# The opening of a two-block transformer kernel: modulation rows moved on TensorE, the first projection chunk split by tokens

## Chip, cores and metric

The kernel runs on one core of a Trainium2 chip. The metric is the device time of one execution in microseconds (us); before the change it is 2401.89 us, the median of three runs (2400.64 to 2404.11). The core has five engines with queues of their own: TensorE (PE, with its weight loads listed apart as PEld), VectorE (DVE), ScalarE (ACT), GpSimd (POOL) and SyncE (SP), which here only issues DMAs. They meet through semaphores alone.

## The reference, cut to what matters

Two diffusion transformer blocks of two layers each run one behind the other on 512 latent tokens of width 1024; the first block also carries 256 context tokens. All is in float32. What the change touches is the beginning of the first block's first layer:

```python
def layer(x, cx, c_silu, cctx_silu, norm_w, ada_w, ada_b, w_in, ...):
    mod = c_silu @ ada_w + ada_b
    mod_c = cctx_silu @ ada_w + ada_b
    shift, scale, gate = jnp.split(mod, 3, axis=-1)
    hx = rmsnorm(x, norm_w) * (1 + scale[:, None, :]) + shift[:, None, :]
    hc = rmsnorm(cx, norm_w) * (1 + scale_c) + shift_c
    px = split_cols(hx @ w_in)
    pc = split_cols(hc @ w_in)
    ...
```

So before the first projection there must be a sum of squares over the 1024 features of each token, its root, and shift and scale, which are products of a vector of 1024 with a matrix of 1024 x 2048, once for the latent and once for the context condition.

## The kernel before

Features lie on the 128 partitions in eight chunks (c = 0 to 7), tokens along the free axis: 512 latent (`SEQ`) and 256 context tokens (`CTX`), 768 in all (`TOK`). Each product of float32 matrices is made of three matmuls of rounded parts: a weight panel is split into its rounded half (made by ACT, `round_panel1`) and the rest (made by DVE for the first two panels, L1958 to L1960, later by POOL); the modulated input h is split in the same way into `hs1[:, 0]` (rounded) and `hs1[:, 1]` (rest). The projection is made in blocks of 128 output features, and `block_chunk` (L2594) adds one chunk c to one block: for the parts (rounded, rounded), (rounded weight, rest of h), (rest of weight, rounded h) it makes one matmul of 512 columns and one of 256.

Every order is written out by hand, as one program per engine; a wait stops all that stands behind it on that engine.

**SP** issues the loads in a row: small vectors, matrices, x in four parts, modulation panels 0 and 1 of 1 MB (`stage_low`), the first two weight panels (`panels_first`, 0.5 MB each), modulation panels 2 to 7, and more.

**PE** begins at L2585 with 36 matmuls of an identity (`WARM_UP`; float32, so two records each), then sums the squares with one-column matmuls (`sum_squares`, L2439: the added squares of seven chunks first, then those of the last chunk), makes the first group of modulation rows (`mod_rows_of(0)`, L2413: two panels of 256 columns, 16 matmuls of 32 output rows each), spreads the roots over the partitions (`spread_roots`, L2563) and turns the rows into columns (`turn_mod(0)`, L2427). There are four such groups g of two panels; group g serves chunks 2g and 2g + 1. In the first block of the projection (L2660 to L2678) the groups 1 to 3 stand between the chunks: rows 1 ahead of chunk 0, turn 1 and rows 2 ahead of chunk 1, turn 2 ahead of chunk 2, rows 3 ahead of chunk 3, turn 3 ahead of chunk 4. Each chunk waits for the rest of h (`h_even` from DVE, `h_odd` from POOL) and then serves the blocks 0 and 1, six matmuls each.

**ACT** squares x, takes the root of the sums (L1555), then makes a small root (L1557), rounds panel 0, copies the rows out of PSUM (`take_rows(0)`, L1333), rounds panel 1, and takes the turned modulation (`take_mod`, L1324). In the loop over chunks (L1564) it adds the shift and rounds: for even chunks in one step per token range (L1584), for odd ones in two (L1575, L1581). Ahead of chunk 2 stand `take_rows(1)`, two `take_mod` and `take_rows(2)`, ahead of chunk 4 two `take_mod`, ahead of chunk 5 `take_rows(3)`; the last two `take_mod` stand within chunk 5.

**DVE** adds the squares (L1955), inverts the roots, makes the rests of panels 0 and 1 (L1960), and then per pair of chunks waits for `mod_taken` and makes shift and gain (`modulate`, L1962, with small additions at L1967). For each chunk it multiplies x by gain and root (L2035, 512 and 256 tokens; `hm_ready`), and after each odd chunk it makes the rest of the even chunk before it (L2041).

**POOL** makes the rest of h for the odd chunks (L1230).

## Time and profile before

| | us |
|---|---|
| median of three runs | 2401.89 |
| lowest and highest run | 2400.64, 2404.11 |
| the profiled execution's own time | 2404.52 |
| its span (first to last instruction) | 2402.4 |
| PE busy | 2345.2 |
| DVE, ACT, POOL busy | 1349.6, 1023.4, 470.7 |

All times below are in us from the start of the span. A timeline row gives start, duration, engine, line and operation, the tile written and the tiles read, the shape, the number of instructions merged into the row, and in brackets how long the engine sat idle before it and what released it. Float32 matmuls leave two records each, those on rounded parts one. Two instructions that follow one another on PE overlap by their tail, so a row of many is somewhat longer than the distance to the next row's start.

### The profile page before, as it was taken

The page shows a single profiled execution, that of the slowest core. Times are in us where ns is not written, and L with a number is a line of the kernel's source. Part 1 is how long each engine was busy: PE and PEld are TensorE (multiplying, and loading weights), DVE is VectorE, ACT ScalarE, POOL GpSimd, SP SyncE. Part 2 cuts the span into 40 slices and gives each one's busy share as a digit, 9 for nine tenths or more (in the row PEclk, how much of TensorE's full clock was granted, in tenths as well). Part 3 has the DMA queues.
Part 4 walks back from the last instruction along what each step waited for, and adds up shares of the span by engine and source line. Part 5 has one row for each costly group of instructions (what it writes and reads, how often), then busy time and mean ns, then how long its engine had stood idle before and what let it go on. Part 6 is the DMA issues. An engine that isn't in the chain of part 4 may idle for free.

```text
span 2402.4 us, 40532 instructions
## 1 busy us (share of the span) xinstructions
PE 2345.2 (98%) x16250; PEld 1943.8 (81%) x16250; DVE 1349.6 (56%) x2719; ACT 1023.4 (43%) x1808; POOL 470.7 (20%) x290
## 2 busy tenths in 40 slices
PE   8999999999999999999999999999999999999998
PEld 6888878788887888878787678888888768888887
DVE  5777675685238755767458644333337855433333
ACT  5673275632337625662454434222235544222222
POOL 2202212012342032203663320000014232000001
PEclk9999999999999999999999999999999999999999
DMA  7303413044133063407242122233232112323222
GB/s 299 141 2 132 167 53 142 2 159 150 60 125 141 2 225 105 150 2 276 90 142 71 62 79 85 83 105 105 81 107 89 62 55 69 108 80 119 96 76 74
DMA packets 64203, 250.55 MB, mean 104 GB/s; under 512 B 7408, under 2 KB 9968, under 8 KB 54544
## 3 DMA queue, kind: packets, MB, share of 16 engines
q1 hardware_dynamic: 61216, 236.10, 28.3%
q0 software_dynamic: 2592, 11.54, 1.5%
q8 instruction: 129, 2.11, 0.3%
q14 instruction: 58, 0.48, 0.1%
q10 hardware_dynamic: 208, 0.33, 0.0%
HBM read 243.67 MB, written 4.19 MB: 103 GB/s over the span
## 4 chain that ended last, share of the span: by engine, by line
PE 84%; ACT 5%; DVE 4%; issue 3%; POOL 2%; DVEq 1%; ACTq 0%; DMA 0%; SPq 0%; POOLq 0%
PE ps L2786 40%; PE ps L2601 21%; PE ps L2763 4%; PE ps L607 4%; PE ps L716 4%; ACT probs L922 3%; PE ps L657 3%; PE ps L701 1%; PE ps L2483 1%; PE ps L2580 1%; POOL split_panels_first L1191 1%; DVEq L805 1%; DVE ps L1944 1%; DVE ps L822 1%; PE ps L2528 1%
## 5 line engine op out<-in xcount | busy, mean ns | idle before, releaser
L2786 PE MATMUL ps<-h_split,split_panels 128*128 128x512 f32 x2928 | 686.1, 393 | 1.9 <-ACT projected L1693 0.8
L2786 PEld LDWEIGHTS ps<-h_split,split_panels 128*128 128x128 f32 x2928 | 545.4, 188 | 126.9 <-issue 14.1
L2601 PE MATMUL ps<-h_split_first,split_panels_first 128*128 128x512 f32 (+1 forms) x2772 | 535.7, 351 | 3.2 <-DVE h_split_first L2041 2.2
L2601 PEld LDWEIGHTS ps<-h_split_first,split_panels_first 128*128 128x128 f32 x2772 | 441.9, 189 | 72.4 <-issue 3.9
L2121 DVE TENSOR_TENSOR split_panels<-panels,split_panels 128x1024 fp32r<-128x1024 f32 (+2 forms) x171 | 191.6, 1121 | 297.3 <-ACT split_panels L1408 293.7
L1191 POOL TENSOR_TENSOR split_panels_first<-panels_first,split_panels_first 128x1024 fp32r<-128x1024 f32 (+2 forms) x102 | 225.2, 2208 | 676.7 <-ACT split_panels_first L1389 676.7
L1408 ACT ACTIVATE split_panels<-panels 128x1024 fp32r<-128x1024 f32 (+2 forms) x210 | 204.3, 974 | 343.0 <-PE ps L2786 341.4
L1944 DVE SCALAR_TENSOR_TENSOR ps<-modulation_panels,silu_c,ps 128x256 f32<-128x256 f32 x480 | 225.3, 488 | 30.0 <-issue 1.7
L2786 PE MATMUL ps<-ffn_hidden_split,split_panels 128*128 128x512 f32 x990 | 225.0, 389 | 0.0
L2786 PEld LDWEIGHTS ps<-ffn_hidden_split,split_panels 128*128 128x128 f32 x990 | 185.8, 188 | 38.6
L1209 POOL TENSOR_TENSOR probs_turned<-probs_turned,probs 128x512 f32<-128x512 f32 x30 | 42.4, 1412 | 760.1 <-ACT probs L1636 760.1
L607 PE MATMUL ps<-qkv 64*128 64x256 f32 (+1 forms) x1232 | 144.8, 362 | 4.5 <-ACT qkv L1470 2.7
L1389 ACT ACTIVATE split_panels_first<-panels_first 128x1024 fp32r<-128x1024 f32 (+2 forms) x104 | 102.9, 990 | 93.9 <-PE ps L2763 93.1
L922 ACT ACTIVATE probs<-ps,row_min 128x512 f32<-128x512 f32 (+6 forms) x192 | 122.1, 643 | 44.1 <-DVE row_min L822 34.0
L1221 POOL TENSOR_TENSOR split_panels<-panels,split_panels 128x1024 fp32r<-128x1024 f32 x39 | 94.3, 2419 | 170.0 <-ACT split_panels L1408 168.8
L2763 PE MATMUL ps<-gated_rounded,split_panels_first 128*128 128x512 f32 x504 | 123.7, 356 | 0.3 <-POOL split_panels_first L1191 0.3
L607 PEld LDWEIGHTS ps<-qkv 64*128 64x128 f32 x1232 | 99.6, 188 | 29.6 <-issue 22.7
L657 PEld LDWEIGHTS ps<-matrices,probs 64*128 64x128 f32 x2048 | 80.9, 139 | 47.3 <-ACT probs L922 42.2
L1468 ACT ACTIVATE qkv<-ps 128x512 f32<-128x512 f32 x38 | 36.3, 954 | 187.0 <-PE ps L2601 186.8
L657 PE MATMUL ps<-matrices,probs 64*128 64x64 f32 x2048 | 92.3, 227 | 19.3 <-ACT probs L922 17.4
L1820 ACT ACTIVATE probs<-ps 128x512 f32<-128x512 f32 x44 | 26.3, 598 | 181.4 <-PE ps L2786 181.3
L2375 DVE TENSOR_TENSOR probs<-probs,ps 128x512 f32<-128x512 f32 x44 | 30.3, 688 | 117.2 <-PE ps L2786 117.2
(313 smaller groups left out, 3071.2 us busy)
## 6 DMA issues: line engine op xcount, KB each, us to landing
modulation_panels<-in_ada SPq DMA_DIRECT2D x64, 1024.0 KB, 4.9
panels<-in_w SPq DMA_DIRECT2D x88, 512.0 KB, 3.2
panels_first<-in_in SPq DMA_DIRECT2D x72, 512.0 KB, 5.7
panels<-in_in SPq DMA_DIRECT2D x42, 512.0 KB, 3.2
panels_first<-in_out SPq DMA_DIRECT2D x32, 384.0 KB, 3.1
panels<-in_w SPq DMA_DIRECT2D x32, 384.0 KB, 3.1
panels<-in_w SPq DMA_DIRECT2D x32, 320.0 KB, 2.9
panels<-in_out SPq DMA_DIRECT2D x16, 512.0 KB, 3.2
```

What stands on the lines that cost most here:

```text
L607: last[e] = nc.tensor.matmul(scores_at(u, e, u["w"][e])[:, col:col + z - a], u["q"][e], u["k"][e][:, a:z], start=True, stop=True, skip_gro ...
L657: ins = [nc.tensor.transpose(to, src, ident[rows_of(half), HD * half:HD * half + HD]) for half, (to, src) in enumerate(two)]
L716: ins = nc.tensor.matmul(bank(b, 0, P)[rows_of(e)], v, turned_slot(ev, at0 + P)[:, at0:at0 + P], start=ev["first"] and j < 2, stop=ev["las ...
L922: nc.scalar.activation(probs[:, u["probs_at"], e, 0:w], scores_at(u, e, w), ACT.Exp, bias=row_min[:, s:s + 1], scale=scale, accum_out=row_ ...
L1191: nc.gpsimd.tensor_tensor(flat1(n, 1)[:, s], raw1[:, n % RAW1, s], flat1(n, 0)[:, s].bitcast(F32), ALU.subtract).then_inc(rest1_done, 1)
L1389: A_(flat1(n, 0)[:, s], raw1[:, n % RAW1, s], ACT.Copy).then_inc(rounded1, 1)
L1408: A_(flat(n, 0), raw[:, n % RAW, 0:panel_size(n)], ACT.Copy).then_inc(rounded, 1)
L1944: ins = V.scalar_tensor_tensor(out=adding if c < KC - 1 else products(k)[:, i, :], in0=w[:, c, :], scalar=v, in1=adding, op0=ALU.mult, op1 ...
L2121: V.tensor_tensor(flat(n, 1), raw[:, n % RAW, 0:panel_size(n)], flat(n, 0).bitcast(F32), ALU.subtract).then_inc(rest_done, 1)
L2601: ins = mm(at0, split1[:, s, w, c, :], hs1[:, h, c, lo:e], start=c == 0 and i == 0, stop=c == KC - 1 and i == 2)
L2763: ins = mm(bank(OUT_BANKS[j][o % 2], 0, e), split1[:, n % SPLIT1, w, c, :], u[:, uc, lo:lo + e], start=uc == 0 and i == 0, stop=uc == MIXC ...
L2786: ins = mm(out, split[:, n % SPLIT, a, c - base, :], moving(b, c), start=first and i == 0 and j == 0, stop=last and i == len(chunks) - 1 a ...
```

## The change

PE: 42 instead of 36 warm-up matmuls. The first group's rows are cut in two: panel 0 goes between the sums of the added squares and those of the last chunk, panel 1 behind them. Behind the first turn stand eight more matmuls of the identity (`SHORT_WAIT`). Block 0's chunks go through a new function, `first_chunk`, which waits only for the rounded h, makes the two parts that need the rounded h, waits for the rest and makes the third. Rows 1 move from ahead of chunk 0 to between its two blocks, rows 2 from ahead of chunk 1 to behind it, turn 2 to between the blocks of chunk 2; turn 1, rows 3 and turn 3 keep their places.

ACT: `take_rows(0)` moves ahead of the small root and the rounding of panel 0; `take_rows(2)` from ahead of chunk 2 to ahead of chunk 3. For chunk 0 the 512 latent tokens wait for a new semaphore, `scaled_first`, which DVE sets after its first product of chunk 0; the 256 context tokens wait for `hm_ready` as before.

```diff
-WARM_UP = 36
+WARM_UP = 42
+SHORT_WAIT = 8
...
                 if l == 0:
                     root(l, TOK // P)
+                    take_rows(0)
+                    round_panel1(0)
                     act.wait_ge(tiny_set, 1)
                     A_(weights_of_squares[:, :], weights_of_squares[:, :], ACT.Sqrt, bias=EPS)
-                    round_panel1(0)
-                    take_rows(0)
                     round_panel1(1)
...
-                    if c == 2:
+                    if c == 3:
                         take_rows(2)
+                    if c == 0:
+                        act.wait_ge(scaled_first, 1)
+                        A_(hs1[:, 0, c, 0:SEQ], hm1[:, c % 4, 0:SEQ], ACT.Identity, bias=mod1[:, l, c, 0:1])
                     act.wait_ge(hm_ready, KC * l + c + 1)
+                    if c == 0:
+                        A_(hs1[:, 0, c, SEQ:TOK], hm1[:, c % 4, SEQ:TOK], ACT.Identity, bias=mod1[:, l, c, 1:2]).then_inc(hh_ready, 1)
+                        continue
...
+                            if (c, j) == (0, 0):
+                                ins.then_inc(scaled_first, 1)
...
-            sum_squares(0, TOK // P)
             pe.wait_ge(silu_done, 3)
-            mod_rows_of(0)
+            sum_added_squares(0, TOK // P)
+            mod_rows_of(0, (0,))
+            sum_last_squares(0, TOK // P)
+            mod_rows_of(0, (1,))
             spread_roots(0, TOK // P)
             turn_mod(0)
+            for _ in range(SHORT_WAIT):
+                mm(bank(0, 0, P), ident, ident, start=True, stop=True)
...
+            def first_chunk(l, b, c):
+
+
+                k, s = NSEQ[l, b], main_no[IN1, l, b] % SPLIT1
+                pe.wait_ge(hh_ready, KC * l + c + 1)
+                for i, (w, h) in enumerate(((0, 0), (1, 0), (0, 1))):
+                    if i == 2:
+                        pe.wait_ge(h_odd if c % 2 else h_even, c // 2 + 1)
+                    for at0, lo, e in ((bank(k % 2), 0, SEQ), (bank(2 + k % 2, 0, CTX), SEQ, TOK)):
+                        ins = mm(at0, split1[:, s, w, c, :], hs1[:, h, c, lo:e], start=c == 0 and i == 0, stop=c == KC - 1 and i == 2)
...
                         pe.wait_ge(rest1_done, main_no[IN1, l, 1] + 1)
+                        (front, front_tokens), (second, second_tokens) = blocks_of(l, m)[0:2]
                         for c in range(KC):
-                            if c == 0:
-                                mod_rows_of(1)
                             if c == 1:
                                 turn_mod(1)
-                                mod_rows_of(2)
-                            if c == 2:
-                                turn_mod(2)
                             if c == 3:
                                 mod_rows_of(3)
                             if c == 4:
                                 turn_mod(3)
-                            pe.wait_ge(h_odd if c % 2 else h_even, c // 2 + 1)
-                            for first, tokens in blocks_of(l, m)[0:2]:
-                                block_chunk(l, first, tokens, c)
+                            first_chunk(l, front, c)
+                            if c == 0:
+                                mod_rows_of(1)
+                            if c == 2:
+                                turn_mod(2)
+                            block_chunk(l, second, second_tokens, c)
+                            if c == 1:
+                                mod_rows_of(2)
                         continue
```

## Rows read from the trace of the kernel before

**Rows 1.** The page, busy time of each engine, share of the span, instructions.

```profile
PE 2345.2 (98%) x16250; PEld 1943.8 (81%) x16250; DVE 1349.6 (56%) x2719; ACT 1023.4 (43%) x1808; POOL 470.7 (20%) x290
```

**Rows 2.** The chain of waits in order of time, opening: start, duration, what.

```profile
14.58 0.97 DVE probs L1955
...
17.09 2.06 PE ps L2446 x12
19.15 3.57 PE ps L2423 x32
...
25.05 0.80 PE ps L2436 x8
```

**Rows 3.** Timeline of PE, 12 to 57 us.

```profile
11.73 2.17 PE L2587 MATMUL ps<-matrices 128*128 128x128 f32 x18
15.59 1.50 PE L2443 MATMUL ps<-matrices,probs 128*128 128x1 f32 x12 [1.69 <-DVE probs L1955]
16.95 2.20 PE L2446 MATMUL ps<-matrices,probs 128*128 128x1 f32 x12
...
25.77 1.07 PE L2423 MATMUL ps<-stage_low,probs_turned 128*32 128x256 f32 x16
...
30.51 3.69 PE L2601 MATMUL ps<-h_split_first,split_panels_first 128*128 128x512 f32 x12 [2.20 <-DVE h_split_first L2041]
...
35.16 1.93 PE L2423 MATMUL ps<-stage_high,probs_turned 128*32 128x256 f32 x32
37.02 2.36 PE L2601 MATMUL ps<-h_split_first,split_panels_first 128*128 128x512 f32 x12
...
46.34 0.95 PE L2436 MATMUL ps<-vectors,probs_turned 128*128 128x2 f32 x8
...
50.45 6.52 PE L2601 MATMUL ps<-h_split_first,split_panels_first 128*128 128x512 f32 x36 [0.96 <-POOL h_split_first L1230]
```

**Rows 4.** Stretches: length, busy of PE, PEld, DVE, ACT, POOL, granted clock, DMA.

```profile
17.51:24.34 6.83, 6.83 (x49) 4.63 (x49) 1.42 (x2) 2.84 (x5) 0.00 (x0) 0.50 1.03 423
...
31.16:34.58 3.42, 3.42 (x14) 2.97 (x13) 0.00 (x0) 0.56 (x2) 1.83 (x1) 0.50 1.01 422
...
705.30:710.80 5.50, 2.34 (x12) 1.64 (x11) 5.03 (x8) 5.21 (x10) 3.60 (x4) 1.00 0.40 152
```

**Rows 5.** Timeline of ACT, opening.

```profile
22.79 0.59 ACT L1339 COPY probs_turned<-ps 128x512 f32<-128x512 f32 x1 [2.30 <-PE ps L2423]
23.27 1.06 ACT L1389 ACTIVATE split_panels_first<-panels_first 128x1024 fp32r<-128x1024 f32 x1
...
28.16 1.12 ACT L1584 ACTIVATE h_split_first<-probs,mod_first 128x512 fp32r<-128x512 f32 x2 [2.06 <-DVE probs L2035]
...
39.84 0.85 ACT L1581 ACTIVATE h_split_first<-probs 128x768 fp32r<-128x768 f32 x1
...
45.43 0.57 ACT L1339 COPY probs_turned<-ps 128x512 f32<-128x512 f32 x1
```

**Rows 6.** The second weight panel's DMA: its issue on SP; size and time to landing.

```profile
5.65 0.47 SPq L1123 DMA_DIRECT2D panels_first<-in_in  x1
...
panels_first<-in_in SPq DMA_DIRECT2D x1, 512.0 KB, 16.6
```

**Rows 7.** Timeline of DVE, 24 to 31 us.

```profile
24.36 1.23 DVE L1960 TENSOR_TENSOR split_panels_first<-panels_first,split_panels_first 128x1024 fp32r<-128x1024 f32 x1 [2.62 <-ACT split_panels_first L1389]
26.20 0.37 DVE L1967 TENSOR_TENSOR mod_first<-mod_first,vectors 128x2 f32<-128x2 f32 x4 [0.61 <-ACT mod_first L1331]
...
26.98 0.75 DVE L2035 SCALAR_TENSOR_TENSOR probs<-qkv,gain_first,ps 128x512 f32<-128x512 f32 x1
...
29.31 1.15 DVE L2041 SCALAR_TENSOR_TENSOR h_split_first<-probs,mod_first,h_split_first 128x512 fp32r<-128x512 f32 x2
```

**Rows 8.** Timeline of POOL and DVE at 40.8 us.

```profile
40.77 1.83 POOL L1230 TENSOR_TENSOR h_split_first<-probs,h_split_first 128x768 fp32r<-128x768 f32 x1 [7.61 <-ACT h_split_first L1581]
...
40.84 1.78 DVE L1967 TENSOR_TENSOR mod_first<-mod_first,vectors 128x2 f32<-128x2 f32 x1 [0.89 <-ACT mod_first L1331]
```

More of the change, by code:

```diff
@@ L370, in two_dit_blocks @@
         silu_done = sem("silu_done")
+        scaled_first = sem("scaled_first")
         part_ready, mod_ready, mod_taken = sem("part_ready"), sem("mod_ready"), sem("mod_taken")
@@ L2411, in _, with mod_rows_of @@
             mm = nc.tensor.matmul
-            def mod_rows_of(g):
+            def mod_rows_of(g, of=(0, 1)):
                 if g >= 1:
                     pe.wait_ge(rows_taken, g)
-                for k in (2 * g, 2 * g + 1):
+                for k in (2 * g + i for i in of):
                     pe.wait_ge(stage_in[k], 16)
@@ L2424, in mod_rows_of @@
                                  start=c < 4, stop=c >= 4, skip_group_check=True)
-                ins.then_inc(rows_ready, 1)
+                if 1 in of:
+                    ins.then_inc(rows_ready, 1)
             def turn_mod(g):
@@ L2437, in turn_mod, with sum_added_squares @@
                     ins.then_inc(mod_ready, 1)
-            def sum_squares(q, blocks):
+            def sum_added_squares(q, blocks):
                 pe.wait_ge(sq_added, 6 * q + 6)
@@ L2443, in sum_squares, with sum_last_squares @@
                     mm(bank(6, SUM_AT + t, SUM_AT + t + 1), square_sum[:, P * t:P * t + P], ones[:, 0:1], start=t == 0, stop=False, skip_group_check=True)
+            def sum_last_squares(q, blocks):
                 pe.wait_ge(sq_ready, KC * q + KC)
@@ L2607, in block_chunk @@
                     ins.then_inc(h_used, 1)
+            def first_chunk(l, b, c):
[6 more added lines that the diff above has]
+                        ins = mm(at0, split1[:, s, w, c, :], hs1[:, h, c, lo:e], start=c == 0 and i == 0, stop=c == KC - 1 and i == 2)
+                if c == KC - 1:
+                    ins.then_inc(proj_ready, 1)
+                elif c == KC // 2 - 1:
+                    ins.then_inc(front_used, 1)
             def blocks_by_parts(l):
```

## The prediction

> **What bounds the kernel now.** I read the page first: TensorE (PE) is busy 98% of the span [rows 1], so only a stretch in which PE waits or runs at half clock has anything to give. The change touches the first 57 us, so the chain of waits in order of time comes next [rows 2]. From 15.59 to 25.85 it is PE alone: two rounds of one-column sums, the first modulation rows, the spread of the norm's roots, the turn of the rows. Then it goes over ACT and DVE until the first projection matmul at 30.51, before which PE sat idle for 2.20 us [rows 3]. Third, stretches cut where the granted clock changes [rows 4]: half (1.2 of 2.4 GHz) from 17.51 to 24.34 and from 31.16 to 34.58, full otherwise. Ahead of the first fall PE was idle for 1.69 us and then ran only one-column sums [rows 2, 3]; ahead of the second came the idle 2.20 us. An idle wait alone doesn't force a fall: from 705.3 to 710.8 PE was busy 2.34 of 5.50 us and kept full clock [rows 4].
>
> 10.25 us at half clock cost at most 5.1 us, and PE's waits of 1.69, 2.20 and 0.96 us [rows 3] add 4.9. The question is how much of this lies on the path.
>
> **The change, part by part.**
>
> *Six more warm-up matmuls* are 12 more records. 18 of them take 2.17 us [rows 3], some 0.11 each with the tail off: 1.35 us more, ending at 15.25. The last adding of squares ends at 14.58 + 0.97 = 15.55 [rows 2], so the idle time covers them. If the clock rose about 1 us later at the start, half of that would stick out past 15.55: 0.3 us at worst.
>
> *Rows between the sums.* In full clock 12 one-column records take 1.36 us (15.59 to 16.95, [rows 3]); 16 row matmuls 1.07 [rows 3], of which some 0.15 is tail. So: sums to 16.95, rows to 18.0, last sums to 19.35, rows to 20.4, spread 12 x 0.11 to 21.75, the turn 0.9 (as at 46.34, [rows 3]) to 22.65. That is 3.2 us ahead of 25.85, provided the clock doesn't fall at 17.51. Between the new root (after 19.45) and the spread lie the second rows, which hide it as they do now.
>
> *ACT's order.* The copy of the rows (0.59, [rows 5]) now stands ahead of the first panel's rounding (1.06, [rows 5]). Copy to 21.1, first rounding to 22.15, then the small root, second rounding from 22.35 to 23.4. It could not start earlier: the second panel was issued at 5.65 and took 16.6 us to land [rows 6], which is 22.25. Behind it DVE makes that panel's rest, 1.23 [rows 7], to 24.7, and DVE's queue holds the modulation behind this rest. So the modulation starts at 24.7, not 0.3 us behind PE's turn, and 1.5 us is gained over 26.20 [rows 7], not 3.2. The wait for PE has turned into one for a panel's landing.
>
> *First chunk by token halves.* DVE needs 0.78 from the modulation to the first product (26.20 to 26.98), then 0.75 for 512 tokens [rows 7]: 26.25. ACT can start on these at once instead of after the 256 as well; its two pieces are 1.12 [rows 5], and the other tokens' product is ready within the first. The rounded half is ready at 27.45, against 29.28: 1.8 gained. DVE's rest ends 3.48 after the first product's start (26.98 to 29.31 + 1.15, [rows 7]), of which a wait of 0.1 goes: 28.9, against 30.46.
>
> *PE from there.* A chunk of both blocks is 12 matmuls, 2.2 us net in full clock (from 37.02, [rows 3]). PE starts at 27.45, does four of block 0's six (0.7), waits for the rest until 28.9, two more to 29.25, then the second rows (1.9, [rows 3]) that used to fill the time before it, and block 1's six: 32.3. Turn: 33.15, against 35.1 now, when the third rows begin [rows 3]. So 2.0 are gained in full clock.
>
> *The idle stretch behind the filler.* Eight filler matmuls are 16 records, 1.8 us: from 22.65 to 24.45. Between 24.45 and 27.45 PE then has nothing: 3.0 us, more than the 2.20 ahead of the fall at 31.16. The nearest row below is the stretch at 705 us, with no fall. So the price of this idle time lies between 0 and 1.7 us (half of a stretch of 3.42, [rows 4]). I take a fall at about 27.75, because 3.0 is nearer to, and beyond, the row that fell. Then the first four matmuls end at 28.6, the rest's two at 29.45, the rows are done at 32.15, the turn at 34.25: 0.85 gained.
>
> *Rows copied at c = 3.* PE's third rows now follow chunk 1, and ACT's copy of them stands ahead of chunk 3's work. From the turn at 34.25: chunk 1 to 36.6, rows to 38.5, copy to 39.05, and only then ACT's 1.12 and 0.85 [rows 5] for chunk 3, so POOL's rest runs from 41.1 to 42.95. Now it runs from 40.77 to 42.60, and DVE's tiny addition beside it takes 1.78 us [rows 8] where four of them took 0.37 [rows 7]: it ends with POOL. Repeated, this makes the modulation of chunks 4 and 5 0.35 later than now, ACT's fourth copy of rows (45.43, [rows 5]) starts at 45.8, and PE's last turn ends at 47.25, against 47.16 now. The early gain is eaten up.
>
> The Trainium skill (SBUF — State Buffer, section "SBUF: two separate sides") says that VectorE and GpSimd share a port pair under an exclusive lock, and that an operation with two SBUF inputs then waits for the other engine's whole instruction. By it the 1.78 us comes back each time, as I have it; were it chance, the last turn would end at 46.65 and the gain would be 0.6 larger.
>
> *The tail.* PE now waits 0.96 us for POOL's rest of chunk 5 [rows 3]. With the rest product last, 0.7 us of other work stands ahead of that wait; some 0.3 is left, and 0.1 goes on the switches. So 0.55 is gained from the last turn to the end at 56.98. Each later chunk has its data in time (chunk 7's rest 7.4 us after the last turn, PE needs it after 7.8).
>
> SP and POOL issue nothing in another order, and the landings follow one another in the queue; no issue waits on what moves. The new wait of ACT for the first product holds only chunk 0 behind it, for which ACT waited anyway.
>
> **Sum.** 0.55 minus 0.1: 0.45 us gained, 2404.07 against the profiled execution's own 2404.52. That one stands 2.63 above the median of the runs shown, 2401.89, so 2401.4 as a median. From 57 us on PE is the bound and the gain is carried through.
>
> **Rivals.**
> *No fall behind the filler.* For it: the stretch at 705 us. PE's turn at 33.15, chunk 1 to 35.4, rows to 37.35; POOL's chunk 3 at 40.05 to 41.9, the fourth copy at 44.7, the last turn at 46.1. 1.05 there and 0.55 in the tail are 1.6: 2400.3, or 2399.7 if the 1.78 doesn't come back. It decides whether PE's clock is still full at 28 us.
> *Slower: the clock still falls at 17.51.* For it: only some 0.5 us of rows runs between the sums and that point, and the first sums are unchanged. Sums and rows then end at 22.85 and the turn at 26.0, but now the copy stands ahead of both roundings: copy to 23.5, roundings to 24.55 and 25.8, DVE's rests to 27.1. Modulation is 0.9 later than now and PE's first matmul waits until 29.8. With a second fall at 31.16 the turn after the second rows ends 2.0 late, without it 0.4. Carried to the end as above, that is 2.4 or 0.8 slower: 2404.3 or 2402.7, in the middle 2403.5. The point that decides is where the second sums run at half clock. The Trainium skill (TensorE: Matmul & The Clock Gate, section "What's actually happening") says that the monitor doesn't restart with a kernel, so the place of a fall varies between executions. By it fixed counts of 42 and 8 fillers would fit some executions only, and this rival would hold in part of them.
> *It doesn't do what it says:* the halves of chunk 0 bring nothing because PE is short of the rest anyway; then 27.45 turns into 28.9, and the second rows stand behind it. That costs 0.7 on the turn after them and as much at the end: 2402.1.
>
> **How the numbers follow.** Likeliest, 0.45: small gain, 2401.4 (its own range 2400.4 to 2402.4). No fall, 0.2: 2400.3. The fall stays, 0.25: 2403.5. Halves idle, 0.1: 2402.1. The runs shown spread over 3.5 us, so each case has about 1 us of play. Range 2398.4 to 2404.0. A measurement of this kernel tells about 0.2% from no change, 4.8 us; no case reaches it: even with full clock throughout, the panel's landing and the 26 us of PE work behind 27.45 leave a gain of 3. What stands outside is noise and a clock fall elsewhere: faster 0.04, slower 0.03, same 0.93.
>
> **What would show it.** Right: the stretch from 17.5 to 24.3 at full clock, the second panel's rounding at 22.3 and DVE's rest ending at 24.7, the first projection matmul near 27.5, a wait of some 0.3 to 0.8 us behind the fourth matmul, an idle stretch of about 3 us ahead, half clock behind it, the last turn near 47, head sums near 56.5. Wrong: half clock between 17.5 and 24 (the slower rival), full clock after 27.7 with head sums near 55.3 (the faster one), a modulation that starts before the second panel's rest, or an end of the opening more than 3 us earlier.

## The result, and the profile after

The changed kernel takes 2407.20 us (median of 20 runs, 2404.14 to 2409.91), the kernel before 2402.09 in the same series (2399.55 to 2405.06): ratio 1.0017, 95% interval [1.0011, 1.0023]. The forecast was 2401.4 and its range ended at 2404.0. The loss is within the 0.2% that the prediction set as "the same", but it is a loss of 5.1 us, and the interval lies wholly above 1. Ratios leave out two runs: one of 4613.89 us among the eleven of a36_three, whose median below counts it, and one of 9520.85 among the 33 of the kernel before beside the first group.

The page of the changed kernel, busy time per engine:

```profile
PE 2350.0 (98%) x16278; PEld 1947.2 (81%) x16278; DVE 1347.9 (56%) x2719; ACT 1025.4 (43%) x1808; POOL 470.7 (20%) x290
```

Against [rows 1] PE has 28 more records (six warm-ups and eight fillers, two each) and 4.8 us more busy time. Some 3 us of it are these records themselves (0.11 each in full clock, [rows 3]), and PE at half clock counts as busy too, so this page alone doesn't say where the loss lies. The timeline of PE in the changed kernel says more (start, duration, line, what, how often, in brackets the idle time before it and who ended it):

```profile
8.68 7.96 PE L2601 MATMUL ps<-matrices 128*128 128x128 f32 x64
16.48 1.40 PE L2454 MATMUL ps<-matrices,probs 128*128 128x1 f32 x12
...
20.24 1.94 PE L2433 MATMUL ps<-stage_low,probs_turned 128*32 128x256 f32 x16
22.10 2.35 PE L2582 MATMUL ps<-matrices,norm_roots 128*128 128x128 f32 x12
24.29 0.95 PE L2447 MATMUL ps<-vectors,probs_turned 128*128 128x2 f32 x8
25.10 2.03 PE L2610 MATMUL ps<-matrices 128*128 128x128 f32 x16
28.91 0.93 PE L2636 MATMUL ps<-h_split_first,split_panels_first 128*128 128x512 f32 x4 [1.77 <-ACT h_split_first L1579]
30.16 0.71 PE L2636 MATMUL ps<-h_split_first,split_panels_first 128*128 128x512 f32 x2 [0.32 <-DVE h_split_first L2051]
30.80 3.46 PE L2433 MATMUL ps<-stage_low,probs_turned 128*32 128x256 f32 x32
...
48.30 1.05 PE L2447 MATMUL ps<-vectors,probs_turned 128*128 128x2 f32 x8 [0.62 <-ACT probs_turned L1341]
...
52.53 0.62 PE L2636 MATMUL ps<-h_split_first,split_panels_first 128*128 128x512 f32 x2 [0.29 <-POOL h_split_first L1232]
...
58.37 1.47 PE L2753 MATMUL ps<-head_of,probs 128*128 128x2 f32 x12
...
62.47 0.60 PE L2594 MATMUL ps<-matrices,probs 128*128 128x1 f32 x4 [0.43 <-DVE probs L1952]
```

Compare with [rows 3]. The 1.69 us of idle time ahead of the sums is gone, yet they start 0.9 later: the warm-ups themselves run until then. The 32 row matmuls of group 1 take 3.46 where 32 of them took 1.93, or twice 1.07: they are at half clock. The last turn, at 46.34 before, is at 48.30, behind a new wait for ACT's copy. The wait for POOL in chunk 5 is 0.29 instead of 0.96, but a wait of 0.43 stands new behind the head's sums.

The stretches of the changed kernel, cut where the granted clock changes (length, then busy time of PE, PEld, DVE, ACT, POOL with counts, the clock, DMA share, GB/s):

```profile
10.00:20.30 10.30, 10.30 (x103) 9.69 (x106) 4.65 (x5) 3.90 (x5) 0.00 (x0) 1.00 1.02 422
20.30:23.70 3.40, 3.40 (x24) 2.16 (x24) 0.19 (x1) 1.65 (x4) 0.00 (x0) 0.50 1.01 422
30.50:33.90 3.40, 3.40 (x34) 1.38 (x32) 0.00 (x0) 0.62 (x1) 1.82 (x1) 0.50 1.02 424
```

The clock fell to half twice, as in [rows 4]: at 20.3, on panel 1's rows and the spread, and at 30.5, on the end of the first matmuls and the rows behind them. The filler at 25.10 did not carry the full clock over to them.

### The profile page after: what moved, and what is told of

It is laid out like the page before. It is cut to its first block, busy times and chain, and to the rows that moved or that the text cites. A ratio compares the mean times of both kernels' runs of the same rounds, so it can differ in the third digit from the quotient of the medians.

```text
span 2405.3 us, 40588 instructions
## 1 busy us (share of the span) xinstructions
PE 2350.0 (98%) x16278; PEld 1947.2 (81%) x16278; DVE 1347.9 (56%) x2719; ACT 1025.4 (43%) x1808; POOL 470.7 (20%) x290
## 4 chain that ended last, share of the span: by engine, by line
PE 84%; ACT 5%; DVE 4%; issue 3%; POOL 2%; DVEq 1%; ACTq 1%; DMA 0%; SPq 0%; POOLq 0%
PE ps L2820 40%; PE ps L2619 20%; PE ps L2797 4%; PE ps L609 4%; PE ps L718 3%; ACT probs L924 3%; PE ps L659 3%; PE ps L703 1%; PE ps L2497 1%; PE ps L2594 1%; PE ps L2661 1%; POOL split_panels_first L1193 1%; DVEq L807 1%; DVE ps L824 1%; PE ps L2601 1%
## 5 line engine op out<-in xcount | busy, mean ns | idle before, releaser
L2619 PE MATMUL ps<-h_split_first,split_panels_first 128*128 128x512 f32 (+1 forms) x2724 | 525.9, 350 | 0.0
L2619 PEld LDWEIGHTS ps<-h_split_first,split_panels_first 128*128 128x128 f32 x2724 | 433.6, 188 | 67.2 <-issue 3.7
L924 ACT ACTIVATE probs<-ps,row_min 128x512 f32<-128x512 f32 (+6 forms) x192 | 122.4, 645 | 43.9 <-DVE row_min L824 33.9
L1828 ACT ACTIVATE probs<-ps 128x512 f32<-128x512 f32 x44 | 26.4, 601 | 181.3 <-PE ps L2820 181.2
L2385 DVE TENSOR_TENSOR probs<-probs,ps 128x512 f32<-128x512 f32 x44 | 30.2, 687 | 117.2 <-PE ps L2820 117.2
```

What stands on the lines that cost most here:

```text
L924: nc.scalar.activation(probs[:, u["probs_at"], e, 0:w], scores_at(u, e, w), ACT.Exp, bias=row_min[:, s:s + 1], scale=scale, accum_out=row_ ...
L2619: ins = mm(at0, split1[:, s, w, c, :], hs1[:, h, c, lo:e], start=c == 0 and i == 0, stop=c == KC - 1 and i == 2)
```

## The experiments

The first four runs ask which part loses, the next four take single parts back, the last four repeat both kernels and cut the change into halves. Each group has its own runs of the kernel before on its chip: their median is 2402.80, 2402.16 and 2402.83 us in this order, against 2402.09 beside the changed kernel. The table gathers what each run's trace shows (us). "Sums late" is from the end of the last addition of squares to the start of the one-column sums; "modulation" is DVE's first small addition; turn g is the turn of group g.

| run | clock rises | half clock in the opening | sums late | addition to modulation | modulation to turn 1 | turn 1 to turn 3 | turn 3 at | own time | median |
|---|---|---|---|---|---|---|---|---|---|
| before | 7.3 | 17.5-24.3, 31.2-34.6 | 0.05 | 10.66 | 7.80 | 12.34 | 46.34 | 2404.52 | 2401.89 |
| b_repeat | 9.7 | 23.4-30.2 | 0.19 | 7.58 | 8.80 | 12.08 | 43.23 | 2404.88 | 2402.52 |
| b_repeat2 | 7.3 | 17.5-21.0 | 0.06 | 9.18 | 6.52 | 12.08 | 42.67 | 2401.26 | 2402.79 |
| after | 10.0 | 20.3-23.7, 30.5-33.9 | 1.46 | 11.06 | 9.26 | 12.96 | 48.30 | 2407.44 | 2407.20 |
| a_repeat | 7.5 | 27.9-31.4 | 0.77 | 9.52 | 9.12 | 12.97 | 46.19 | 2404.90 | 2407.05 |
| b_warm42 | 8.2 | 18.4-21.8, 28.7-32.1 | 0.73 | 9.66 | 8.01 | 12.07 | 44.54 | 2405.64 | 2405.64 |
| stage_ab | 9.2 | 19.4-29.7 | 1.42 | 12.18 | 6.51 | 12.08 | 45.45 | 2406.57 | 2406.48 |
| loop_only | 10.1 | 27.2-30.6 | 0.52 | 8.42 | 9.24 | 12.97 | 45.25 | 2404.01 | 2405.06 |
| a_warm36 | 9.4 | 26.4-29.9 | 0.14 | 8.96 | 8.39 | 12.95 | 45.39 | 2406.57 | 2405.01 |
| a36_copy2 | 9.8 | 26.9-30.3 | 0.40 | 9.15 | 8.74 | 12.26 | 44.79 | 2405.38 | 2404.33 |
| a36_rows1 | 9.7 | none | 0.42 | 9.16 | 5.60 | 13.02 | 42.39 | 2403.58 | 2403.64 |
| a36_round | 9.9 | 26.9-30.4 | 0.30 | 8.53 | 9.01 | 12.96 | 45.30 | 2403.77 | 2404.62 |
| a36_three | 7.4 | 17.6-24.5 | 0.15 | 10.93 | 5.59 | 12.15 | 43.48 | 2404.63 | 2401.78 |
| halves_only | 7.8 | 18.1-21.5 | 0.15 | 9.24 | 5.57 | 12.17 | 42.04 | 2402.85 | 2402.86 |

### The kernel before, once more (b_repeat)

No edit.

> The kernel before, unchanged, as a control and for a second profile. Every theory: ratio 1.000 within 0.001. If the place at which the clock rises differs between executions, this profile's rise during the warm-up lies elsewhere than at 7.27 us, and its falls elsewhere than at 17.51 and 31.16; if it is tied to the kernel, they lie within 0.3 us of these.

Measured: 2402.52, ratio 0.9995 [0.9986, 1.0004]. Its opening is another one than in [rows 2 to 4]: the clock rises at 9.7, not 7.3, stays full over sums, rows and turn, and the last turn is 3.1 us earlier. The profile on which the prediction rests was thus one opening of several. The timeline of PE in this run:

```profile
8.62 6.50 PE L2587 MATMUL ps<-matrices 128*128 128x128 f32 x52
14.96 1.40 PE L2443 MATMUL ps<-matrices,probs 128*128 128x1 f32 x12
...
23.65 1.94 PE L2423 MATMUL ps<-stage_low,probs_turned 128*32 128x256 f32 x16 [1.76 <-DMA stage_low<-in_ada]
```

There is no idle time between the 36 warm-ups and the sums: with a late rise they fill the wait exactly, and six more can only push the sums back.

### The number of warm-ups (a_warm36, b_warm42)

a_warm36 is the changed kernel, b_warm42 the kernel before:

```diff
-WARM_UP = 42
+WARM_UP = 36
```
```diff
-WARM_UP = 36
+WARM_UP = 42
```

> The changed kernel with 36 warm-up matmuls again. Theory W (the longer warm-up pushes the sums past the last adding of squares): the sums start at 15.6 instead of 16.48 and about 0.9 us of the 5.1 come back; all of it if W is the whole cause. Theory L (the loop over chunks with the rows behind chunk 1 is the cause): the start comes back but the end of the first chunks hardly moves, less than 0.5 us.

> The kernel before with 42 warm-up matmuls and nothing else. Theory W: slower by 0.5 to 1 us where the clock rises late (sums start near 16.4), more if the later sums also push the clock's fall over the rows. Theory L: within 0.3 us of before.

Measured: 2405.01, ratio 1.0009 [1.0000, 1.0018], and 2405.64, 1.0006 [0.9997, 1.0015]. Taking six away from the changed kernel gives back about half of its loss (0.0008 of 0.0017). These are the middle values: the intervals of the changed kernel with 42 and with 36 (1.0011 to 1.0023, 1.0000 to 1.0018) overlap. Adding six to the kernel before costs 0.0006, and its interval still holds no change. The sums start 0.73 to 1.46 us behind the last addition in the four runs with 42 warm-ups, and 0.05 to 0.52 in the ten with 36.

### The first stage alone (stage_ab)

The kernel before with the warm-ups, the rows between the sums and ACT's order of the change, its loop as it was:

```diff
-WARM_UP = 36
+WARM_UP = 42
...
+                    take_rows(0)
+                    round_panel1(0)
                     act.wait_ge(tiny_set, 1)
...
-                    round_panel1(0)
-                    take_rows(0)
...
-            sum_squares(0, TOK // P)
             pe.wait_ge(silu_done, 3)
-            mod_rows_of(0)
+            sum_added_squares(0, TOK // P)
+            mod_rows_of(0, (0,))
+            sum_last_squares(0, TOK // P)
+            mod_rows_of(0, (1,))
```

> Only the first stage of the change: 42 warm-up matmuls, rows cut between the sums, the copy of rows ahead of the roundings; the loop over chunks as before and no filler matmuls. Theory W: slower than before by 0.5 to 1 us or more. Theory L: equal to before or up to 2 us faster, and the whole 5 us come from the loop.

Measured: 2406.48, ratio 1.0009 [1.0000, 1.0018]. The stage that was to be faster is about 2 us slower by itself, by an interval that begins at no change. In its profile the clock falls at 19.4, in spite of the rows between the sums, and stays at half for 10.2 us; the modulation comes 12.18 behind the last addition, the longest of all.

### Single parts taken back, with 36 warm-ups (a36_copy2, a36_rows1, a36_round, a36_three)

All four start from a_warm36. a36_copy2 puts the third rows (those of group 2) back ahead of chunk 1 and ACT's copy of them back ahead of chunk 2; a36_rows1 puts the second rows (group 1) back ahead of chunk 0 and leaves the filler out; a36_round rounds panel 0 ahead of the copy again; a36_three does all three and puts turn 2 back, so that rows between the sums, token halves and the rest product last remain.

```diff
-                    if c == 3:
+                    if c == 2:
                         take_rows(2)
...
                                 turn_mod(1)
+                                mod_rows_of(2)
...
-                            if c == 1:
-                                mod_rows_of(2)
```
```diff
-SHORT_WAIT = 8
+SHORT_WAIT = 0
...
-                            first_chunk(l, front, c)
                             if c == 0:
                                 mod_rows_of(1)
+                            first_chunk(l, front, c)
```
```diff
-                    take_rows(0)
                     round_panel1(0)
+                    take_rows(0)
```

> The changed kernel with 36 warm-up matmuls, and rows 2 and ACT's copy of them back at the places of the kernel before (rows behind turn 1, copy ahead of chunk 2). Theory C (the copy ahead of chunk 3 delays ACT, POOL and DVE behind it): from the start of turn 1 to the start of turn 3 it takes 12.1 us as in the kernel before, not 12.95, and PE's wait of 0.6 us for the fourth copy goes; about 0.9 us less in all than with the 36 matmuls alone. Rival (the stretch is PE's own work in another order): 12.9 stays.

> The changed kernel with 36 warm-up matmuls, rows 1 back ahead of chunk 0 and no filler matmuls. Theory R (rows 1 used time in which PE had nothing to do; behind the first matmuls they lie on the path): from the first modulation on DVE to the start of turn 1 it is 1 us shorter or more than the 8.4 with the 36 matmuls alone, unless half clock lies on it. Rival (the filler kept the clock up and earns what the rows cost): the same 8.4 or longer, with half clock in chunk 0.

> The changed kernel with 36 warm-up matmuls, and ACT rounds panel 0 ahead of the copy of the rows again. Theory A (that rounding was free beside PE's rows, and behind the copy it delays DVE's rests and so the modulation): DVE's second rest ends 1 us earlier relative to the end of the first rows (3.2 us behind it, not 4.2), and the modulation begins when PE's turn is done. Rival (the second panel's landing bounds it): the second rest ends no earlier than 2.4 us behind that landing, and nothing is gained.

> All three together with turn 2 back as well: 36 warm-up matmuls, no filler, rows 1 and 2, turn 2, the copy and the rounding at their old places; of the change only the rows between the sums, the chunk by token halves and the rest product last remain. If theories W, C, R and A hold and their shares add up, this is as fast as the kernel before or up to 1.5 us faster (ratio 0.9995, within 0.001). If a rest of the change costs by itself, it stays 1 us or more slower than before.

Measured: 2404.33, 1.0010 [1.0001, 1.0019]; 2403.64, 1.0005 [0.9996, 1.0013]; 2404.62, 1.0012 [1.0003, 1.0021]; 2401.78, 0.9997 [0.9988, 1.0006]. By ratio none of the single parts can be told from a_warm36 (1.0009) within the intervals; all three together return the time to that of before. The traces tell the parts apart better. With the copy back at c = 2, turn 1 to turn 3 is 12.26 in place of 12.95. With panel 0 rounded first (a36_round), addition to modulation is 8.53 in place of 8.96, and no more is to be had there, because ACT then waits for the second panel's landing (ACT's timeline in a36_round):

```profile
21.10 1.06 ACT L1391 ACTIVATE split_panels_first<-panels_first 128x1024 fp32r<-128x1024 f32 x1 [0.41 <-DMA panels_first<-in_in]
```

With the second rows back, modulation to turn 1 is 5.60 in place of 8.39, and the clock stays full (PE's busy time and the clock up to 60 us in a36_rows1):

```profile
9.70:60.00 50.30, 46.03 (x390) 37.72 (x389) 32.34 (x72) 29.74 (x59) 14.02 (x10) 1.00 0.80 317
```

PE is idle there too, but on both sides of row matmuls (its timeline):

```profile
23.96 1.07 PE L2433 MATMUL ps<-stage_low,probs_turned 128*32 128x256 f32 x16 [1.78 <-DVE split_panels_first L1968]
26.18 1.07 PE L2433 MATMUL ps<-stage_low,probs_turned 128*32 128x256 f32 x16 [1.15 <-DMA stage_low<-in_ada]
27.18 1.32 PE L2636 MATMUL ps<-h_split_first,split_panels_first 128*128 128x512 f32 x6
```

In all six profiles with the filler the clock went to half between 0.4 us before and 1.6 us after the first matmul that follows it (in the changed kernel at 30.5, that matmul being at 28.91). The rows in the wait are the better filler: they are work that has to be done. But they don't always hold the clock either: it fell at 23.4 in b_repeat, just ahead of the first of them, and at 31.2 in the profiled kernel before and 28.7 in b_warm42, where the first matmul behind them had waited 2.20 and 1.50 us. It did not fall there in b_repeat2 and a36_three, where that wait was 1.22 and 1.01, nor in a36_rows1 and halves_only, which had none. No run moved the rows without adding the filler, so what each of the two costs by itself is not shown.

### Both kernels again, and the change in two halves (a_repeat, b_repeat2, loop_only, halves_only)

a_repeat and b_repeat2 are unaltered. loop_only is the changed kernel with the first stage undone; halves_only is the kernel before with `first_chunk` and `scaled_first` alone, all rows, copies and warm-ups where they were.

```diff
-WARM_UP = 42
+WARM_UP = 36
...
-                    take_rows(0)
-                    round_panel1(0)
...
+                    round_panel1(0)
+                    take_rows(0)
...
-            mod_rows_of(0, (0,))
...
-            mod_rows_of(0, (1,))
+            mod_rows_of(0)
```
```diff
+                            first_chunk(l, front, c)
+                            block_chunk(l, second, second_tokens, c)
-                            for first, tokens in blocks_of(l, m)[0:2]:
-                                block_chunk(l, first, tokens, c)
```

> The changed kernel once more, unaltered, to see what of its loss belongs to the program and what to the one profiled execution. My theory (the loss is made of the opening's parts: six more warm-ups that delay the sums, the copy ahead of the roundings, the filler that does not hold the clock, the copy at c = 3, and a tail whose gain is partly handed back): the parts that depend on no clock recur to a few hundredths, so the second ones of the turns are 12.95 us behind the first (before 12.1), the head's sums 10.06 behind the last turns (before 10.64), and the first sum of the modulation's chunk behind them waits 0.43 us for VectorE. If the clock rises at 9 us or later, the sums start over 1 us behind the last addition, and the half clock comes before 21 us. Ratio 1.0017, between 1.0007 and 1.0027. Rival (the loss is that of executions with an unlucky clock, and another series would not show it): ratio within 0.9990 to 1.0007.

> Before, with the token halves of the first chunk and its rest product last alone; all else, the filler (none) and warm-ups (36) too, as before. My theory: the two parts that are good by themselves remain. First turns to last turns as before (12.1 us), the head's sums 9.95 to 10.07 behind the last turns in place of 10.64, the first chunk's matmuls 1 to 1.8 us sooner behind the modulation than in the run before of like clock, and 0.43 us handed back where the first sum behind the head's waits for VectorE. Ratio 0.9996, between 0.9986 and 1.0006. Rival (the rest product last is what makes the first chunk of the changed kernel late, since it waits for GpSimd's rounding at the end): ratio 1.0007 or more, with TensorE's wait for GpSimd or VectorE between the first chunk's products over 1 us.

> The changed kernel with its first stage undone: 36 warm-ups, the one-column sums unsplit, the modulation rows behind them as before, the copy behind the roundings as before. What remains are the moved rows and filler behind the first chunk, the copy at c = 3, and the token halves. My theory (first stage about 2.5 us of the loss, loop about 2): from modulation to the second turns 8 us or more, with idle time of 1.8 us or more on TensorE behind the filler and a half clock after it unless the clock was already half before; first to last turns 12.95, wait behind the head's sums 0.43. Ratio 1.0008, between 0.9998 and 1.0018. Rival (the first stage carries all of the loss): 0.9998 or less. Rival (the loop carries all of it): 1.0015 or more.

> The kernel before once more, as the measure of what two series of one program differ by beside the other three, and of where its clock rises in another execution. Every theory expects 1.0000 within 0.0010, first to last turns 12.1 us, the head's sums 10.64 behind, and no wait of the first sum behind them. The rise of the clock is expected anywhere from 7.3 to 10 us; if it comes at 9 or later, the sums start within 0.3 us of the last addition and the first half clock comes behind 22 us; if at 8 or earlier, the half clock comes by 18.5.

Measured: a_repeat 2407.05, 1.0017 [1.0008, 1.0025]; halves_only 2402.86, 0.9998 [0.9990, 1.0007]; loop_only 2405.06, 1.0008 [0.9999, 1.0017]; b_repeat2 2402.79, 0.9998 [0.9990, 1.0007]. The loss recurs in another series. By the middle values the first stage (stage_ab) and the loop carry about half of it each, 1.0009 and 1.0008; the interval of either reaches from no change to the whole loss. The parts that hang on no clock recurred within a few hundredths. The clock of a_repeat rose at 7.5, so what was expected of a late rise was not seen in it again.

That makes a_repeat and b_repeat2 a pair with like starts: the clock rises at 7.5 and 7.3, and the modulation begins at 24.10 and 24.07. Here is the latter in DVE's timeline of b_repeat2 (the former is shown further down):

```profile
24.07 0.37 DVE L1967 TENSOR_TENSOR mod_first<-mod_first,vectors 128x2 f32<-128x2 f32 x4
```

First the timeline of PE in b_repeat2, the kernel before:

```profile
24.25 1.07 PE L2423 MATMUL ps<-stage_low,probs_turned 128*32 128x256 f32 x16 [0.66 <-DVE split_panels_first L1960]
26.10 1.07 PE L2423 MATMUL ps<-stage_low,probs_turned 128*32 128x256 f32 x16 [0.78 <-DMA stage_low<-in_ada]
28.39 2.37 PE L2601 MATMUL ps<-h_split_first,split_panels_first 128*128 128x512 f32 x12 [1.22 <-DVE h_split_first L2041]
30.59 0.95 PE L2436 MATMUL ps<-vectors,probs_turned 128*128 128x2 f32 x8
...
42.67 0.95 PE L2436 MATMUL ps<-vectors,probs_turned 128*128 128x2 f32 x8
...
56.82 0.53 PE L2580 MATMUL ps<-matrices,probs 128*128 128x1 f32 x4
```

and the same of a_repeat, the changed kernel:

```profile
22.36 2.03 PE L2610 MATMUL ps<-matrices 128*128 128x128 f32 x16
26.93 0.93 PE L2636 MATMUL ps<-h_split_first,split_panels_first 128*128 128x512 f32 x4 [2.53 <-ACT h_split_first L1579]
28.18 1.01 PE L2636 MATMUL ps<-h_split_first,split_panels_first 128*128 128x512 f32 x2 [0.32 <-DVE h_split_first L2051]
29.12 3.01 PE L2433 MATMUL ps<-stage_low,probs_turned 128*32 128x256 f32 x32
32.06 1.33 PE L2619 MATMUL ps<-h_split_first,split_panels_first 128*128 128x512 f32 x6
33.22 0.95 PE L2447 MATMUL ps<-vectors,probs_turned 128*128 128x2 f32 x8
...
46.19 1.05 PE L2447 MATMUL ps<-vectors,probs_turned 128*128 128x2 f32 x8 [0.61 <-ACT probs_turned L1341]
...
60.35 0.61 PE L2594 MATMUL ps<-matrices,probs 128*128 128x1 f32 x4 [0.43 <-DVE probs L1952]
```

Both kernels can go on only when the rest of h is there, at 28.39 and 28.18: the token halves bring it 0.2 us sooner. From there before needs 2.20 to turn 1, because the second rows lie in the wait ahead; the changed kernel needs 5.04, of which 2.94 are those rows, on the path and mostly at half clock. That is 2.6 us. Turn 1 to turn 3 costs 0.89 more, of which 0.61 is the wait for the copy. From turn 3 to the sum behind the head's both take the same, 14.15 and 14.16. Sum: 0.03 + 2.60 + 0.89 + 0.01 = 3.53, the distance of the last rows of the two timelines; the executions' own times lie 3.64 apart, the medians of their series 4.26.

halves_only shows what is left of the gain. Its half-clock stretch is like that of b_repeat2 (18.1 to 21.5); modulation to turn 1 is 5.57 in place of 6.52, the head's sums come 9.96 behind turn 3 in place of 10.65, and PE waits 0.45 behind them. Of 0.95 gained at turn 1, 0.1 goes in the switches up to turn 3; the runs cannot tell the rest from nothing. No run beat the kernel before by more than the intervals allow, so no version is offered.

## Why the prediction was wrong, step by step

In short, the changed kernel did nearly what the prediction's chain said, once; but the kernel before reached its last turn over 3 us sooner in two other profiles than in the one it was compared with.

**The step that failed first: "That one stands 2.63 above the median of the runs shown, 2401.89, so 2401.4 as a median."** The forecast was made against the profiled execution and then moved by 2.63 as if that excess lay elsewhere. It lay in the opening itself, in the part that the change replaces. b_repeat2 has its last turn at 42.67, not 46.34, 3.67 earlier, and its own time is 3.26 lower. Three things had made the profiled opening slow: the last addition ended at 15.54 (14.58 to 15.09 in all other runs), the first half clock lasted 6.8 us (3.4 in b_repeat2), and a second one fell at 31.2 (none in b_repeat2). With that second fall, turn 1 came 7.80 behind the modulation; without it 6.52. The gain on that turn ("So 2.0 are gained in full clock") was reckoned from this delayed turn: the forecast 33.15 is later than the 31.54 at which turn 1 ended in b_repeat2.

**The chain itself was right for one execution.** Forecast and a_repeat: modulation to the first rounded half 2.75 and 2.83; to the rest 4.2 and 4.08; idle time behind the filler 3.0 and 2.53; the fall at 27.75 and 27.9; turn 1 ending at 34.25 and 34.17; the last turn ending at 47.25 and 47.24; head sums at 56.5 and 56.25. The clock did not fall at 17.5 there, with rows between the sums and a rise at 7.5. But this was the fastest of the 11 runs of that program, 2.15 below its median, so the agreement is in part luck: in the other profile of the same program the clock rose at 10.0 and the last turn began at 48.30. One sum in the chain slipped: two of twelve matmuls that take 2.2 us in full clock need 0.73 at half, so the rest's two would have ended at 29.63, not 29.45; the end of the rows moves by 0.1.

**Six more warm-ups, "so the idle time covers them"**, was wrong: the sums start 0.73 to 1.46 us late in place of 0 to 0.3. The cover was the idle 1.69 us of [rows 3], which a late addition and an early rise had made; b_repeat has none.

**Rows between the sums** held the clock in one of the three profiles that have them with 42 warm-ups: full until 27.9 in a_repeat, half from 19.4 in stage_ab and from 20.3 in the changed kernel. With 36 and an early rise they did not hold it (a36_three, 17.6). With 36 and a late rise it held until 26.4 or later in four runs that have them, but also until 23.4 and 27.2 in two that don't (b_repeat, loop_only). The slower rival, a fall on the second sums, had the right kind: in the profiled run it came 2.8 us later, on the rows and the spread. Whether more rows there would hold it was not tried.

**ACT's order** was priced too low. "The wait for PE has turned into one for a panel's landing" was to start the modulation 2.45 behind the landing. The second panel landed at 21.01 in a_repeat, and the modulation began 3.09 behind. What binds there is ACT's queue with the copy ahead of both roundings (ACT's timeline in a_repeat):

```profile
20.25 0.59 ACT L1341 COPY probs_turned<-ps 128x512 f32<-128x512 f32 x1 [0.85 <-PE ps L2433]
20.73 1.06 ACT L1391 ACTIVATE split_panels_first<-panels_first 128x1024 fp32r<-128x1024 f32 x1
21.69 0.20 ACT L1561 ACTIVATE weights_of_squares<-weights_of_squares 128x8 f32<-128x8 f32 x1
21.79 1.04 ACT L1391 ACTIVATE split_panels_first<-panels_first 128x1024 fp32r<-128x1024 f32 x1
```

DVE's two rests follow from 21.82 without a gap for 2.36, and the modulation behind them (DVE's timeline in a_repeat):

```profile
21.82 2.36 DVE L1968 TENSOR_TENSOR split_panels_first<-panels_first,split_panels_first 128x1024 fp32r<-128x1024 f32 x2 [2.13 <-ACT split_panels_first L1391]
24.10 0.36 DVE L1975 TENSOR_TENSOR mod_first<-mod_first,vectors 128x2 f32<-128x2 f32 x4
```

In b_repeat2 the first of them was made at 19.89 while PE was still at the rows. So a turn that was ready 1.1 us earlier (21.55 against 22.64) gave a modulation that was no earlier at all. With the copy behind the first rounding again (a36_round) the landing does bind, and the modulation follows it by 2.26.

**The copy at c = 3** was right: a loss of 0.94 from turn 1 to turn 3 forecast, 0.89 measured, and a36_copy2, which takes it back, has 12.26 in place of 12.95. The tiny addition that ends with POOL recurs (DVE, then POOL, in a_repeat):

```profile
40.97 2.00 DVE L1975 TENSOR_TENSOR mod_first<-mod_first,vectors 128x2 f32<-128x2 f32 x4 [2.25 <-ACT mod_first L1333]
```
```profile
40.90 1.84 POOL L1232 TENSOR_TENSOR h_split_first<-probs,h_split_first 128x768 fp32r<-128x768 f32 x1 [9.87 <-ACT h_split_first L1589]
```

By the Trainium skill (SBUF — State Buffer, section "SBUF: two separate sides") the two engines share a port pair under an exclusive lock; the trace agrees, with 2.00 us for what took 0.37 alone, in b_repeat2 as well.

**The tail, "So 0.55 is gained from the last turn to the end at 56.98"**, was right up to there and wrong in what follows. The head's sums do come 0.57 sooner behind turn 3 (10.06 to 10.07, before 10.64). But 4 us on, a one-column sum waits for products that DVE makes behind POOL's rest of chunk 7. In b_repeat2 the last of these, in DVE's timeline, ends 0.13 ahead of that sum (56.82):

```profile
56.21 0.48 DVE L1944 SCALAR_TENSOR_TENSOR probs<-modulation_panels,silu_c,ps 128x256 f32<-128x256 f32 x1
```

PE and DVE arrive there together, so PE alone can gain 0.13. In all 14 profiles the way from turn 3 to that sum takes 14.05 to 14.17 us. The tail is not a term at all: what counts is when turn 3 comes.

**The rival that the halves bring nothing** was nearly right: the rest comes 0.2 sooner. Its price of 0.7 was too small, since it too was reckoned from the delayed turn of [rows 3], which hid that the rows moved behind the rest cost their length.

**The clock's place** was taken from one trace and carried as a chance of 0.25. The Trainium skill (TensorE: Matmul & The Clock Gate, section "What's actually happening") says that the monitor doesn't restart with a kernel; that agrees with rises from 7.3 to 10.1 in the 14 profiles. That variation should have stood ahead of the sum: every count of fillers was fitted to one of these starts. The stretch at 705 us [rows 4] was one sight of many, too. It holds two waits of PE, 1.72 and 0.95 us; the same two stand between 700 and 711 us in all 14 profiles, and in the 13 others the clock fell there, 1.0 to 2.6 us behind the start of the matmul that ends the first wait. In b_repeat2 that matmul (PE's timeline) and the stretch at half clock behind it are:

```profile
702.49 0.94 PE L2628 MATMUL ps<-h_split_first,split_panels_first 128*128 128x512 f32 x3 [1.72 <-DVE h_split_first L2012]
```
```profile
703.60:710.40 6.80, 6.02 (x16) 4.97 (x17) 5.98 (x8) 5.00 (x10) 5.67 (x5) 0.50 0.96 325
```

So the sentence "An idle wait alone doesn't force a fall" rested on the one execution of the 14 in which the clock did not fall there, and so did the rival "No fall behind the filler" with its 0.2.

What stays open is how often each opening comes: there is one profile per run, and the timed runs have no trace. So the 5.1 us are not split exactly; the like pair explains 3.6, and the first stage costs more where the clock rises late (1.46 at the sums, a fall at 20.3), which may account for the rest; no run shows that it does.

## What to carry to other kernels

When the profiled execution stands above the median, find out in which stretch its excess lies before a change of that stretch is credited against it; one unaltered repeat does that. Work that lies in a wait costs nothing there and its whole length elsewhere: moving 1.9 us of rows out of the wait for the rest cost 2.6, mostly at half clock, and a filler in their place did not keep the clock. A gain on PE counts only up to the next point at which another engine arrives at the same time, so follow the chain past the end of the changed stretch.

## What the runs showed of the hardware

The same program met quite different clocks: in three profiles of the kernel before, full clock came at 7.3, 9.7 and 7.3 us and first ended at 17.5, 23.4 and 17.5; in two of the changed one it came at 10.0 and 7.5 and first ended at 20.3 and 27.9. Behind the opening the same holds: from the sum behind the head's to the end are 2341.9 to 2342.8 us in some executions and 2344.4 to 2345.4 in others, of the kernel before as of the variants, which is a good part of the spread of the runs. The granted clock goes with it: leaving out the last 10 us, the six shorter ones spent 3.4 or 6.8 us of this way at half clock, the eight longer ones 13.7 or 17.1. So two executions of the kernel before (the profiled one and b_repeat) differ by 3.5 us in a part that no edit touched. Keeping PE busy did not by itself keep the clock: in stage_ab it was busy all the way through the stretch before the fall and through the half-clock stretch after it:

```profile
9.20:19.40 10.20, 10.20 (x100) 9.60 (x99) 4.80 (x6) 4.33 (x6) 0.00 (x0) 1.00 1.03 426
19.40:29.70 10.30, 10.30 (x73) 7.08 (x72) 5.21 (x13) 3.87 (x9) 0.00 (x0) 0.50 1.01 419
```
